# Delta scan: quadrants of one inverse product, and the order of seeds, outputs and far products between tiles

## The reference, cut to what matters

```python
a_mat = where(strict_lower, (k * beta) @ k.T * decay, 0)
t_mat = triangular_solve(eye + a_mat, eye)          # the inverse of I + A
u = t_mat @ (v * beta)
w = t_mat @ (k * beta * exp(gc))
# then, chunk after chunk:
v_new = u - w @ s
o = q_dec @ s + qk @ v_new
s = s * g_last + k_dec.T @ v_new
```

## Time and profile before

| | |
|---|---|
| median of 3 runs | 2659.38 us |
| the runs | 2656.29 to 2664.13 us |
| the profiled execution's span | 2659.2 us |
| granted TensorE clock, mean | 0.993 |
| TensorE matmul busy | 2564.7 us (96%) |
| TensorE weight loads busy | 2153.5 us (81%) |
| VectorE busy | 1649.2 us (62%) |
| ScalarE busy | 782.7 us (29%) |
| GpSimd busy | 1181.4 us (44%) |

### The profile page before, as it was taken

The page is one execution under the profiler, slowest core; times in us unless marked ns, Lnnn a source line. Parts: engine busy times, 40 slices in busy tenths (PEclk is TensorE's granted clock), DMA queues, the critical chain, the costliest instruction groups (busy, mean ns, idle before and its releaser), DMA issues. The chain is left out here.

```text
span 2659.2 us, 45976 instructions
## 1 busy us (share of the span) xinstructions
PE 2564.7 (96%) x18832; PEld 2153.5 (81%) x18832; DVE 1649.2 (62%) x2479; ACT 782.7 (29%) x1373; POOL 1181.4 (44%) x938
## 2 busy tenths in 40 slices
PE   8999999999899999999899989999899999999998
PEld 6878888888678888878788879876798888788887
DVE  7869849651668939767655466544787326772451
ACT  3224214221334303333544254322464100220000
POOL 3545554555335455523431253222443445554553
PEclk9999999999999999999999999999999999999999
DMA  4233334232024433322011110111211322222222
GB/s 164 89 117 142 121 142 143 92 107 95 1 79 158 146 123 142 108 75 74 27 43 50 48 42 27 35 39 49 57 25 54 105 95 95 80 95 95 95 96 78
DMA packets 51175, 229.47 MB, mean 86 GB/s; under 512 B 5280, under 2 KB 12464, under 8 KB 32432
## 3 DMA queue, kind: packets, MB, share of 16 engines
q1 hardware_dynamic: 50992, 226.84, 24.6%
HBM read 224.65 MB, written 2.17 MB: 85 GB/s over the span
## 5 line engine op out<-in xcount | busy, mean ns | idle before, releaser
L246 POOL TENSOR_TENSOR ring_rounded<-ring,ring_rounded 128x512 fp32r<-128x512 f32 (+2 forms) x711 | 951.2, 1369 | 1049.1 <-DVE ring_rounded L237 760.5
L300 PE MATMUL psum<-arena_rounded,ring_rounded 128*128 128x512 f32 (+1 forms) x2820 | 1093.3, 388 | 32.4 <-DVE arena_rounded L651 10.2
L301 PE MATMUL psum<-arena_rounded,ring_rounded 128*128 128x512 f32 (+1 forms) x2820 | 1084.3, 385 | 0.0
L302 PE MATMUL psum<-arena_rounded,ring_rounded 128*128 128x512 f32 (+1 forms) x2820 | 1084.0, 384 | 0.0
L300 PEld LDWEIGHTS psum<-arena_rounded,ring_rounded 128*128 128x128 f32 x2820 | 531.9, 189 | 148.9 <-issue 25.7
L302 PEld LDWEIGHTS psum<-arena_rounded,ring_rounded 128*128 128x128 f32 x2820 | 531.7, 189 | 106.1
L301 PEld LDWEIGHTS psum<-arena_rounded,ring_rounded 128*128 128x128 f32 x2820 | 532.2, 189 | 103.1 <-issue 1.0
L237 DVE CAST ring_rounded<-ring 128x2048 fp32r<-128x2048 f32 (+5 forms) x134 | 145.2, 1083 | 475.8 <-PE psum L302 458.5
L849 ACT ACTIVATE arena<-psum,vectors 128x512 f32<-128x512 f32 x88 | 67.9, 772 | 257.4 <-DVE psum L889 257.4
L262 ACT ACTIVATE ring_rounded<-ring 128x2048 fp32r<-128x2048 f32 (+1 forms) x57 | 104.6, 1835 | 100.4 <-PE psum L302 65.5
L2208 DVE SCALAR_TENSOR_TENSOR arena<-psum,vectors,arena 128x510 f32<-128x510 f32 (+3 forms) x160 | 95.9, 638 | 12.2 <-ACT arena L2134 9.7
(11 more groups left out here) (455 smaller groups left out, 3274.0 us busy)
## 6 DMA issues: line engine op xcount, KB each, us to landing
ring<-in_w_up SPq DMA_DIRECT2D x44, 1024.0 KB, 4.8
arena<-in_w_mod SPq DMA_DIRECT2D x48, 512.0 KB, 5.5
ring<-in_w_down SPq DMA_DIRECT2D x32, 704.0 KB, 4.1
ring<-in_w_mup SPq DMA_DIRECT2D x16, 1024.0 KB, 4.8
ring<-in_w_mdown SPq DMA_DIRECT2D x16, 1024.0 KB, 4.9
ring<-in_w_gdn SPq DMA_DIRECT2D x12, 1024.0 KB, 4.8
ring<-in_w_lru_in SPq DMA_DIRECT2D x10, 1024.0 KB, 5.0
ring<-in_w_odd_in SPq DMA_DIRECT2D x10, 1024.0 KB, 4.8
```

What stands on the lines that cost most here:

```text
L246: last = pool.tensor_tensor(self.rounded(low), raw, self.rounded(high).bitcast(F32), ALU.subtract)
L300: pe.matmul(out, r(wh), r(xh), start=start, stop=False)
L301: pe.matmul(out, r(wh), r(xl), start=False, stop=False)
L302: return pe.matmul(out, r(wl), r(xh), start=False, stop=stop)
```

## The change

It does five things. (1) The Z products of direction 1 take their inputs from the other half of the partitions, so that they use the off-diagonal quadrants, and the loop takes the four quadrants in turn, as the X products do. The Z bank of direction 1 then holds its halves swapped, and its `z_copy` becomes two copies of 64 partitions that swap them back. (2) `seed` is split. `seed_left` (the X bank) stands behind `far_left` and ahead of the outputs; `seed_right` (the Z bank, in the four quadrants in turn) stands behind direction 0's output. (3) `far_right` comes next, and direction 1's output behind it. (4) On ScalarE the X copies of the next tile's seeds come ahead of the far copies. (5) The work beside a level goes into a function `beside(t, k, d)`, for TensorE and VectorE, called for direction 0 and then 1; on VectorE it now stands ahead of `dve_kept`.

```diff
-        def seed(t):
+        def seed_left(t):
             for d in range(2):
                 pe.wait_ge(sem("z1", d), count("z1", d, t + 1))
                 if t:
-                    pe.wait_ge(sem("zdiag", d), count("zdiag", d, t))
                     pe.wait_ge(sem("xcopy", d), count("xcopy", d, 6 * t))
...
+        def seed_right(t):
             for d in range(2):
-                for r in half:
-                    pe.matmul(m.psum[r, scan_bank(d, ZB), 0:GH * HB], m.ident[r, r],
-                              B[d]["Z1"][r].rearrange("p a b -> p (a b)"), start=True, stop=False, skip_group_check=True)
+                if t:
+                    pe.wait_ge(sem("zdiag", d), count("zdiag", d, t))
+            for i in range(2):
+                for d in range(2):
+                    z = place(d, i)
+                    pe.matmul(m.psum[half[i], scan_bank(d, ZB), 0:GH * HB], m.ident[z, z],
+                              B[d]["Z1"][z].rearrange("p a b -> p (a b)"), start=True, stop=False, skip_group_check=True)
...
-            for d in range(2):
-                for h in range(GH):
-                    for r in half:
-                        last = pe.matmul(compact(d, ZB)[r, h, :], B[d]["YC"][r, h, :], z[d][r, h, :], start=False,
+            for h in range(GH):
+                for i in range(2):
+                    for d in range(2):
+                        y = place(d, i)
+                        last = pe.matmul(compact(d, ZB)[half[i], h, :], B[d]["YC"][y, h, :], z[d][y, h, :], start=False,
                                          stop=False, skip_group_check=True)
-                last.then_inc(up("zmul", d), 1)
+                        if h == GH - 1 and i == 1:
+                            last.then_inc(up("zmul", d), 1)
...
+        seed_left(0)
+        seed_right(0)
         for t in range(NA):
-            seed(t)
             for k in range(1, LEVELS + 1):
...
             far_left(t, 0)
             far_left(t, 1)
+            if t + 1 < NA:
+                seed_left(t + 1)
             if t - 1 >= 2:
                 output(t - 1, 0)
-                output(t - 1, 1)
+            if t + 1 < NA:
+                seed_right(t + 1)
             far_right(t, 0)
             far_right(t, 1)
+            if t - 1 >= 2:
+                output(t - 1, 1)
...
             if k < LEVELS:
-                act.activation(B[d]["ZC"], compact(d, ZB), ACT.Copy).then_inc(up("zcopy", d), 1)
+                if d == 0:
+                    last = act.activation(B[d]["ZC"], compact(d, ZB), ACT.Copy)
+                else:
+                    for i in range(2):
+                        last = act.activation(B[d]["ZC"][place(d, i)], compact(d, ZB)[half[i]], ACT.Copy)
+                last.then_inc(up("zcopy", d), 1)
                 return
...
             for i in range(2):
-                last = act.activation(B[d]["ZF"][half[i], :, half[i]], compact(d, ZB)[place(d, i)], ACT.Copy)
+                last = act.activation(B[d]["ZF"][half[i], :, half[i]], compact(d, ZB)[half[i]], ACT.Copy)
...
+        x_copy(0, 0, 0)
+        x_copy(0, 0, 1)
         for t in range(NA):
-            x_copy(t, 0, 0)
-            x_copy(t, 0, 1)
...
+            if t + 1 < NA:
+                x_copy(t + 1, 0, 0)
+                x_copy(t + 1, 0, 1)
             far_copy(t, 0)
             far_copy(t, 1)
...
+                beside(t, k, 0)
+                beside(t, k, 1)
                 if (t, k) == (2, 2):
                     m.dve_kept(dve)
```

More of the change, by code:

```diff
@@ L2570, in query_spread, with beside @@
             last.then_inc(m.up("qspread"), 1)
+        def beside(t, k, d):
+            if (t, k) in ((0, 5), (1, 1)):
+                query_spread(2 * t + d)
+            if k == 1 and t >= 2:
+                state_product(t - 1, d)
+            if k == 2 and 2 <= t + 1 < NA:
+                query_gram(t + 1, d)
+            if k == 3 and t + 1 < NA:
+                gram(t + 1, d)
+            if k == 4 and t:
+                inverse_product(t - 1, d)
+            if k == 5 and t:
+                state_update(t - 1, d)
         m.hold(pe, 16, scan_bank(0, YB))
+        seed_left(0)
+        seed_right(0)
         for t in range(NA):
-            seed(t)
             for k in range(1, LEVELS + 1):
@@ L2580, in pe @@
                     query_turn()
-                if (t, k) in ((0, 5), (1, 1)):
-                    query_spread(2 * t)
-                    query_spread(2 * t + 1)
-                for d in range(2):
-                    if k == 1 and t >= 2:
-                        state_product(t - 1, d)
-                    if k == 2 and 2 <= t + 1 < NA:
-                        query_gram(t + 1, d)
-                    if k == 3 and t + 1 < NA:
-                        gram(t + 1, d)
-                    if k == 4 and t:
-                        inverse_product(t - 1, d)
-                    if k == 5 and t:
-                        state_update(t - 1, d)
+                beside(t, k, 0)
+                beside(t, k, 1)
                 right(t, k)
@@ L2807, in dve, with beside @@
         triangle(0, 1)
+        def beside(t, k, d):
+            if (t, k) in ((0, 5), (1, 1)):
+                query_scaled(2 * t + d)
+            if k == 1 and t >= 2:
+                residual(t - 1, d)
+            if k == 2 and 2 <= t + 1 < NA:
+                query_weights(t + 1, d)
+            if k == 3 and t + 1 < NA:
+                triangle(t + 1, d)
+            if k == 4 and t:
+                updates(t - 1, d)
+            if k == 5 and t:
+                state(t - 1, d)
         for t in range(NA):
@@ L2817, in dve @@
                     query_roots()
+                beside(t, k, 0)
+                beside(t, k, 1)
                 if (t, k) == (2, 2):
                     m.dve_kept(dve)
-                if (t, k) in ((0, 5), (1, 1)):
-                    query_scaled(2 * t)
-                    query_scaled(2 * t + 1)
-                for d in range(2):
-                    if k == 1 and t >= 2:
-                        residual(t - 1, d)
-                    if k == 2 and 2 <= t + 1 < NA:
-                        query_weights(t + 1, d)
-                    if k == 3 and t + 1 < NA:
-                        triangle(t + 1, d)
-                    if k == 4 and t:
-                        updates(t - 1, d)
-                    if k == 5 and t:
-                        state(t - 1, d)
             negate(t, 0)
```

## The result

| | before | after |
|---|---|---|
| median, 20 runs each, taken in turn | 2661.02 us | 2666.85 us |
| range of the runs | 2656.29 to 2665.87 | 2660.63 to 2672.17 |
| span of the profiled execution | 2659.2 | 2666.7 |
| granted clock in it, mean | 0.993 | 0.990 |
| TensorE matmul busy | 2564.7 | 2547.1 |

The ratio is 1.002, with a 95% interval of 1.0014 to 1.0027. The forecast was 2658.1 us (2651 to 2664); the changed kernel takes 2666.85 us, slower than before by more than noise and by less than 0.3%.

A forecast was written before the change was run, and what follows sets the result against it. It took TensorE as the likely bound, its weight loads busy for 86% of the delta scan's two runs. Terms 0 + 0.7 - 0.4 - 1.7 + 0.1 = -1.3 us gave 2658.1 us, range 2651 to 2664.

The forecast's parts named there:

- Z products by quadrants: TensorE, each level: 0.43 us saved, 25.6 in all, but worth 0 because `left` waits for ScalarE's X copies.
- The clock is no rival: Whole stage: granted clock stays at 1.00, since no level after the change is as empty as 6.43 of ten microseconds.
- Split Z copies: ScalarE, direction 1's copy in halves: about +0.3 us per level, felt only at tile 0, two groups x 0.35 = +0.7.
- Rival 3: ScalarE's queue: dearer half copies delay level 2's X copy, placed at level 1 of tiles 0 to 4; 2663.4 us, 8%.
- Transitions without outputs: After tiles 0, 1, 2, six in all: seeds ahead, `left` at +4.49 against mean 4.56, -0.07 each, -0.4 us.
- Transitions with outputs: After tiles 3 and 4, four in all: `left` at +7.38 instead of 7.81 us, gain 0.43 each, -1.7 us.
- The bound of -0.85 each: Best case per transition after tiles 3 and 4: no cost of changing between quarter and full array.
- The last tile: Tile 5: outputs split the same way without seeds, -0 to +0.4, taken +0.05 each, +0.1 us.
- Issue waits: TensorE's "issue" waits, before `left` and other lines, may move or vanish: within 3.6 us, in the range, no own case.
- The sum: All terms over both scans added: 0 + 0.7 - 0.4 - 1.7 + 0.1 = -1.3 us.
- The test that the prediction named: Forecast is wrong if X to `left` shrinks below 1.5 us, or both scans together move by over 4 us.

The follow-up runs named there:

- halves_only: Kernel before with one edit: ScalarE copies the second direction's Z as two activations of 64 partitions instead of one of 128; 2663.6 us, ratio 1.0012.
- order_only: Changed kernel with Z seeds and products back on the diagonal quadrants and whole Z copies, leaving only the new order; 2660.2 us, ratio 0.9991.
- short_first_seed: Kernel before with the very first Z seeds of each scan issued for direction 0 alone; 2663.3 us, ratio 1.0004.

## Why the prediction was wrong

- **Z products by quadrants, 0 on the path: right.** X to `left` stayed at 1.55 us (where it can be read: 48 levels have a `left` right behind them, not 60). Z fell to 39.2 us busy (43 forecast), and the weight loads of `left` wait 29.7 us for ScalarE's X copies (30 forecast).
- **The clock is no rival: this is the step that failed.** It reasoned from one window of before with its loads busy for 6.43 of ten microseconds at 1.00, and said that after the change no level is that empty. The same ten microseconds of the changed kernel have the loads busy for 4.47. In it tile 0 fell to the 1.2 GHz level six times. The old kernel has a stretch with 5.70 at 1.00 as well (1295 to 1305), so the emptiness of such a stretch decides nothing by itself. Over the runs the mean clock is 0.99115 against 0.99289, which by 2.03 us for each 0.001 is 3.5 of the 5.9 us by which the means differ. The same time saved on TensorE that was rightly worth nothing on the path was thus not free: the first seeds end 0.42 us earlier, TensorE stands still before `left`, the old kernel with this gap alone lost 0.0010 of clock, and filling the gap in the changed kernel brought back 3.7 us, of which its clock (0.9921) explains 1.9. What else is needed for a fall is open, since six of twelve such gaps had none behind them.
- **Split Z copies, +0.7: mechanism right, half of it missing.** The copies take 0.44 us more per level (1.09 against 0.65 us from the first Z copy to what follows it), not 0.3. At tile 0, before `left` of level 3 (the place of the earlier trace rows), they cost 0.42 and 0.57 instead of 0.35 each: +1.0. Levels 2 to 4 were called free because nobody waits for the Z copies themselves; behind them in ScalarE's queue stands the query exponential, behind that GpSimd's product, and beside that the 64x256 products of VectorE's `triangle` slow down: 3 x 0.43 = +1.3. Together 2.3 us, and halves_only by itself showed 2.5. Rival 3 named the queue but the wrong place, level 1.
- **Transitions without outputs, -0.4:** 4.55 in the changed kernel against a mean of 4.56; worth 0. Without waits for "issue" it was 4.48 before, so the new order itself costs 0.07 where -0.07 was forecast.
- **Transitions with outputs, -1.7: right** (7.32 us against 7.38; 4 x -0.49 = -2.0, though in this profile the fourth was taken back by its longer seeds). The bound of -0.85 each was wrong in kind: more was to be had not from free changes of mode but from leaving the seeds on two quadrants (0.76 us each in order_only).
- **The last tile, +0.1:** from Z's first start in level 5 to the end of the last outputs it is 14.50 us in both kernels; 0.
- **Issue waits, within 3.6 us: right as a bound, wrong as a remark.** In the changed kernel they came out equal (3.3 against 3.4 us). But in single profiles a change of placement alone moved them by 2.9 to 4.3 us, as much as the whole change moved the time.
- **The sum.** At an equal clock: +2.3 - 2.0 + 0 = +0.3 us by the steps, +2.4 (standard error 0.5) by the runs; the rest of 2.1 us isn't traced, and is less than the 2.5 us that a mere shift of the instructions moved. With the clock's 3.5 us this is the +5.9.
- **The test that the prediction named** ("if both scans together move by over 4 us") was met, +9.5 us from the first `left` to the last Z products of each, and pointed at the right stage.

## What to carry to other kernels

Work that is saved where an engine waits anyway is worth nothing on the path, and on TensorE it can cost: list the stretches that become emptier, and look at the granted clock there after the change before trusting a zero. A step added to a queue is priced by everything behind it in that queue, over engines (here ScalarE to GpSimd to VectorE's slower `triangle`), not by its own consumer. With effects of 0.1 to 0.2%, put a few harmless instructions ahead of the stage in both versions: what changes by that is no gain or loss of the edit.

## What the runs showed of the hardware

- The granted clock of the stage depends on small gaps, in a way that neither busy share nor gap length orders. Standing still for 0.41 us before the first `left` went with a fall in the changed kernel and, at 0.42 us, with none at that place in short_first_seed. In halves_only the same wait before `left` of level 3 went with none in the first group (1.00 over 1295 to 1297) and with one in the second (0.50 over 1574 to 1576), as its two rows below show. A fall in tile 0 of the changed kernel cost 1.3 to 1.6 us of the path each time.

```profile
1295.18 0.76 PE L2460 MATMUL psum<-arena 64*64 64x64 f32 x32 [2.10 <-ACT arena L2613]
...
1573.27 0.81 PE L2460 MATMUL psum<-arena 64*64 64x64 f32 x32 [2.09 <-ACT arena L2613]
```

- Products of 64x64 on off-diagonal quadrants run beside 256-column products on the diagonal ones: 1.01 us for both groups, against 1.33 us when both groups want all four. The Trainium skill (TensorEngine Tiling, Tiling Modes) describes four tiles that work in parallel, and this agrees: what counts is which quadrants two neighbouring groups take, not only how many one of them uses.
- VectorE's two 64x256 products in `triangle`, with both inputs in SBUF, take 0.85 us with GpSimd idle, 1.26 and 1.69 us with GpSimd's 128x512 product beside them for the first 0.54 and 0.96 us. So 0.41 and 0.84 us more for 0.54 and 0.96 us of overlap: these products hardly move while GpSimd's runs. The 128x128 products just ahead of them, with one input in PSUM, are not held up: three take 0.86 us beside it, four take 1.12 us with GpSimd idle.
- With eight products of one column ahead of the scan, TensorE's issue waits read 6.3 instead of 3.4 us in one kernel and 7.6 instead of 3.3 in another, one profile each.
